# Hybrid block kernel: the second half of the modulation is summed on VectorE, and ScalarE evicts every projection result

## What is computed

```
m = silu(cond) @ w_ada + b_ada          # cond: two vectors, w_ada: 1024 x 6144
sh1, sc1, g1, sh2, sc2, g2 = split(m, 6)
h = rmsnorm(x, norm_mix) * (1 + sc1) + sh1
gq, gk, gv, gg, glr, sq, sk, sv = split(h @ w_in)      # 1024 x 2848
g_f, g_b = log_sigmoid(glr @ w_gk + b_gk) / 16         # gates, then running sums
sq, sk = rotary(rmsnorm(sq)), rotary(rmsnorm(sk))
x = x + g1 * merge(gla(gq, gk, gv, g_f, g_b), gg, attention(sq, sk, sv))
h = rmsnorm(x, norm_ff) * (1 + sc2) + sh2
x = x + g2 * (relu(h @ w_ff1) ** 2 @ w_ff2)
```

## Time and profile before

| | |
|---|---|
| runs of the kernel before, median of 3 | 1648.76 us (1645.47 to 1649.05) |
| the profiled execution, its own time | 1647.43 us |
| span of the profiled execution | 1645.7 us |
| projection stage, about | 40 to 388.4 us of the span |
| TensorE busy over the span | 1588.2 us (97%) |
| VectorE busy over the span | 973.5 us (59%) |

### The profile page before, as it was taken

The page is one execution under the profiler, slowest core; times in us unless marked ns, Lnnn a source line. Parts: engine busy times, 40 slices in busy tenths (PEclk is TensorE's granted clock), DMA queues, the critical chain, the costliest instruction groups (busy, mean ns, idle before and its releaser), DMA issues.

```text
span 1645.7 us, 31938 instructions
## 1 busy us (share of the span) xinstructions
PE 1588.2 (97%) x11618; PEld 1391.1 (85%) x11618; DVE 973.5 (59%) x1503; ACT 687.3 (42%) x1212; POOL 1019.1 (62%) x784
## 2 busy tenths in 40 slices
PE   4999999998999999999999999999999999999998
PEld 1999778897788877788889899998979899998987
DVE  2713564775665665457866656666694545545468
ACT  2513323324454566213444444444535444444441
POOL 1711455573485799103777777687898767676673
PEclk7999999999999999999999999999999999999999
DMA  8344555749655763334743132331344132231313
GB/s 323 109 131 165 187 181 191 264 143 257 195 162 171 230 179 114 147 130 155 215 167 103 51 102 63 90 95 58 103 132 150 52 102 73 80 102 51 102 52 115
DMA packets 211450, 225.93 MB, mean 137 GB/s; under 512 B 52752, under 2 KB 171664, under 8 KB 208144
## 3 DMA queue, kind: packets, MB, share of 16 engines
q1 hardware_dynamic: 209248, 224.46, 42.9%
q10 hardware_dynamic: 2096, 0.02, 0.1%
HBM read 177.22 MB, written 47.24 MB: 136 GB/s over the span
## 4 chain that ended last, share of the span: by engine, by line
PE 44%; POOL 4%; DVE 1%; issue 1%; ACT 0%; DMA 0%; SPq 0%; DVEq 0%; ACTq 0%; POOLq 0%
PE ff_banks L3189 8%; PE ff_banks L3190 8%; PE ff_banks L3191 8%; PE ff_banks L3162 7%; PE ff_banks L3164 7%; PE ff_banks L3163 7%; POOL h_whi L2835 1%; POOL h_xop L2432 1%; POOL h_wlo L2847 1%; POOL h_whi L2842 1%; DVE ff_tmp L3036 0%; DMA ff_hb<-in_w_ff 0%; DVE ff_acc L3026 0%; DVE ff_acc L2993 0%; POOL h_wlo L2882 0%
## 5 line engine op out<-in xcount | busy, mean ns | idle before, releaser
L3162 PE MATMUL ff_banks<-h_xop,h_whi 128*128 128x320 f32 x888 | 275.2, 310 | 4.6 <-POOL h_whi L2835 2.0
L3164 PE MATMUL ff_banks<-h_xop,h_whi 128*128 128x320 f32 x888 | 274.4, 309 | 0.0
L3163 PE MATMUL ff_banks<-h_xop,h_whi 128*128 128x320 f32 x888 | 274.3, 309 | 0.0
L2993 DVE TENSOR_TENSOR ff_acc<-ff_acc,ff_banks 128x512 f32<-128x512 f32 x296 | 200.6, 681 | 100.5 <-PE ff_banks L3191 98.9
L3189 PE MATMUL ff_banks<-h_wlo 128*128 128x512 f32 x580 | 226.5, 390 | 1.6 <-POOL h_whi L2842 0.8
L3191 PE MATMUL ff_banks<-h_wlo 128*128 128x512 f32 x580 | 225.6, 389 | 0.0
L2835 POOL TENSOR_TENSOR h_whi<-mid_raw,h_whi 128x512 fp32r<-128x512 f32 x149 | 208.4, 1415 | 1.4 <-ACT h_whi L2687 1.4
L2847 POOL TENSOR_TENSOR h_wlo<-mid_raw,h_wlo 128x320 fp32r<-128x320 f32 x128 | 116.7, 913 | 127.4 <-ACT mid_raw L2724 127.4
L3162 PEld LDWEIGHTS ff_banks<-h_xop,h_whi 128*128 128x128 f32 x888 | 166.7, 188 | 8.3 <-issue 3.6
L3163 PEld LDWEIGHTS ff_banks<-h_xop,h_whi 128*128 128x128 f32 x888 | 166.7, 188 | 1.1
L3164 PEld LDWEIGHTS ff_banks<-h_xop,h_whi 128*128 128x128 f32 x888 | 166.7, 188 | 0.0
(11 more groups left out here) (323 smaller groups left out, 3771.6 us busy)
## 6 DMA issues: line engine op xcount, KB each, us to landing
mid_raw<-in_w_ff SPq DMA_DIRECT2D x124, 512.0 KB, 4.4
mid_raw<-in_w_ada SPq DMA_DIRECT2D x18, 1024.0 KB, 7.2
early_room<-qk_by_channel SPq DMA_DIRECT2D x20, 512.0 KB, 4.2
proj<-prj_stage SPq DMA_DIRECT2D x60, 152.0 KB, 1.9
mid_raw<-in_w_in SPq DMA_DIRECT2D x6, 1216.0 KB, 7.3
early_room<-in_w_ada SPq DMA_DIRECT2D x6, 1024.0 KB, 11.1
decays<-early_room SPq DMA_DIRECT2D x8, 640.0 KB, 4.6
early_room<-decays SPq DMA_DIRECT2D x20, 256.0 KB, 2.9
```

The lines of the kernel that those rows point to most:

```text
L2993: dve.tensor_tensor(acc[:, p, at], acc[:, p, at], down[n % RING], ALU.add).then_inc(added, 1)
L3162: pe.matmul(out, w_hi[:, k], x_hi[:, k], start=(k == 0), stop=False)
L3163: pe.matmul(out, w_hi[:, k], x_lo[:, k], start=False, stop=False)
L3164: mm = pe.matmul(out, w_lo[:, k], x_hi[:, k], start=False, stop=(k == KH - 1))
```

## The change

The modulation's sixteen later slices are no longer multiplied on TensorE. Their 4096 columns are taken as four quarters of 1024 columns (u = 0 to 3: g1, sh2, sc2, g2). A quarter is loaded in four pieces of two slices (256 rows by 1024 columns, as many bytes as one slice before), two pieces in each of groups 2 to 9. For each slice and each of the two conditioning vectors VectorE multiplies 128 x 1024 weights with the vector's 128 values, one for each partition, and adds the product to a running sum (`dve_later`: 64 instructions, of which the 8 that begin a sum only multiply). When a quarter is complete, TensorE adds up the 128 partitions with a matrix that has one column of ones (`pe_sum`: four matmuls, after items 37, 49, 65 and 80). Rows, transposes and picks follow once for each quarter. All items from 10 on are evicted by ScalarE; `evacuate` is gone from VectorE.

```diff
+    def dve_later(self, dve, i, k, j, count):
+        u, q = i // 4, i % 4
+        dve.wait_ge(self.later_in[j], 16 * count)
+        for c in range(2):
+            t = 4 * i + 2 * k + c
+            by = self.silu[:, 2 * q + k, c:c + 1]
+            in_ = self.raw_slice(j)[:, 2 * k * HALF:(2 * k + 2) * HALF]
+            if t % 16 < 2:
+                if u:
+                    dve.wait_ge(self.sum_ready, u)
+                op = dve.tensor_scalar(self.sums[:, c], in_, by, None, ALU.mult)
+            else:
+                dve.wait_ge(self.product_ready, t - 1)
+                op = dve.scalar_tensor_tensor(self.sums[:, c], in_, by, self.sums[:, c], ALU.mult, ALU.add)
+            op.then_inc(self.product_ready, 1)
+
+    def pe_sum(self, pe, bank, u):
+        pe.wait_ge(self.picked, 3)
+        pe.wait_ge(self.product_ready, 16 * (u + 1))
+        if u:
+            pe.wait_ge(self.rows_ready, u + 1)
...
+        for c, j, row, at in self.places(u):
+            mm = pe.matmul(bank[row - c:row - c + 32, :], self.pick[:, c], self.sums[:, c, j * HALF:(j + 1) * HALF], start=True, stop=True)
+        mm.then_inc(self.sum_ready, 1)
...
-        slices = [(g, at) for g, places in ((2, (3, 7)), (3, (2, 5)), (4, (2, 5)), (5, (2, 5)), (6, (5,)), (7, (2, 5, 9)), (8, (1, 5, 9)), (9, (4,))) for at in places]
...
+        for g in range(2, NG):
+            for m, (load, first) in enumerate(((0, 1), (3, 4)) if by_channel(g) else ((-3, -1), (1, 3)) if g == NG - 1 else ((0, 2), (5, 7))):
+                i = 2 * (g - 2) + m
+                slice_load_at[FIRST_ITEM[g] + load] = i
+                for k in range(2):
+                    slice_at[FIRST_ITEM[g] + first + k] = (i, k)
...
+        sum_at = {FIRST_ITEM[4] + 1: 0, FIRST_ITEM[6] + 1: 1, FIRST_ITEM[8] + 1: 2, FIRST_ITEM[9] + 6: 3}
+        rows_at = {n + 1: u for n, u in sum_at.items()}
...
-        def on_act(n):
-
-            return n < NT or n % 2 == 1
...
                         if used_until[g - 1]:
-                            sp.wait_ge(ada.slice_used, KD + used_until[g - 1])
+                            sp.wait_ge(ada.product_ready, 4 * used_until[g - 1])
...
                     if n == max(heads_at) + 6:
-                        sp.wait_ge(ada.slice_used, 3 * KD)
+                        sp.wait_ge(ada.product_ready, 8 * KD)
...
-                        if on_act(n):
-                            evacuate(n)
+                        evacuate(n)
...
-                    elif not on_act(n):
-                        evacuate(n)
...
+                    if n in slice_at:
+                        i, k = slice_at[n]
+                        ada.dve_later(dve, i, k, slices[i] % 2, slice_count[i])
```

More of the change, by code:

```diff
@@ new lines, in dve_later_rows, with dve_later_pick @@
+    def dve_later_rows(self, dve, bank, u):
+        dve.wait_ge(self.sum_ready, u + 1)
+        dve.wait_ge(self.bias_in, 16 * 4 * (u + 2))
+        dve.tensor_tensor(self.rows[:, :], bank, self.rows[:, :], ALU.add).then_inc(self.rows_ready, 1)
+    def dve_later_pick(self, dve, bank, u):
+        cols = bank.rearrange("p (b j r) -> p j b r", j=4, r=32)
+        dve.wait_ge(self.cols_ready, u + 1)
+        for c in range(2):
+            src = cols[:, 2 * c:2 * c + 2, :, c]
+            if u == 1:
+                dve.tensor_copy(self.keep["shift"][:, 1].rearrange("p (j b) c -> p j b c", j=2)[:, :, :, c], src).then_inc(self.shift_ready, 1)
+            else:
+                gain = self.gain[:, 1].rearrange("p (j b) -> p j b", j=2)
+                dve.scalar_tensor_tensor(self.keep["scale"][:, 1].rearrange("p (j b) c -> p j b c", j=2)[:, :, :, c], src, 1.0, gain,
+                                         ALU.add, ALU.mult).then_inc(self.scale_ready, 1)
@@ L229, in dve_pick, with sp_store @@
                     dve.scalar_tensor_tensor(out[:, jj], src[:, jj], 1.0, gain, ALU.add, ALU.mult).then_inc(self.scale_ready, 1)
[L231 to L236, removed]
+    def sp_store(self, sp, u):
+        sp.wait_ge(self.rows_ready, u + 2)
+        for c, j, row, at in self.places(u):
+            sp.dma_start(self.scratch["mod"][c:c + 1, at:at + HALF], self.rows[row:row + 1, :]).then_inc(self.mod_out, 16)
 class HeadNorm:
@@ L763, in _ @@
                         i = slice_load_at[n]
-                        room = slices[i][0]
+                        room = slices[i]
                         sp.wait_ge(wlo_ready, room)
-                        sp.wait_ge(ada.slice_used, KD + (i if room == g else used_until[room - 2]))
-                        ada.sp_later(sp, 1 + i // KD, i % KD, room % 2)
+                        before = i if i % 2 else used_until[room - 2]
+                        if before:
+                            sp.wait_ge(ada.product_ready, 4 * before)
+                        ada.sp_later(sp, i, room % 2)
                     store(n)
```

102 lines of the change are left out of this document (51 added, 51 removed).

## The result

The changed kernel takes 1676.56 us in the median of five runs (1676.45 to 1678.31), against 1648.76 us before: ratio 1.0184, with a 95% interval of 1.0172 to 1.0197. It is 28 us slower; forecast were 13 us, and the range ended at 1674. One execution of the kernel before at 3292.3 us is left out of the comparison.

The account below looks back on a forecast made before the run. TensorE bounds the kernel overall, but VectorE is full in the projection's last groups. The stage would end at 401.5 us instead of 388.4, 13.1 us later: 1647.4 + 13.1 = 1660.5, against the median 1662; range 1647 to 1674.

Parts of the forecast that it names:

- The step that failed: Groups 2 to 6: VectorE's 40 products, some 45 us, roughly fit 56 us of waits; scan of item 53 at about 275.3.
- the way that the prediction had named itself: Around item 51: item 49's eviction 7.4 us earlier moves group 7's high and low parts; VectorE goes on at 268.1.
- the prediction's own signs of being wrong: Fourth sum finds products ready, products run at half of 1.2 us, or TensorE's idle ends on an eviction or weights' part.
- Late pieces: Group 9: pieces take 7.2 us to land, hidden behind some 12 us of VectorE work; if not, a few us at most.
- TensorE's part: Projection stage: sixteen slices, 17.05 us, go and four sums, 4.3 us, come; net 12.8 us less, the whole possible gain.
- shorter stops ... around items 51 and 65: TensorE at sums and transposes around items 51 and 65 to 67: stops of some us, taking only part of the same lag.
- VectorE full from item 53 to its last product: From the scan at 275.3 us VectorE works 113.6 us without a wait for data or TensorE; last product at 388.9.
- The last sum and behind: TensorE idles 10 to 20 us before the fourth sum, then 1.1 + 10.0 + 1.5 us to the stage's end at 401.5.
- Evictions at nothing: ScalarE's 37 more evictions, 5 us more in the last three groups, cost nothing, since TensorE has four banks.
- SyncE's loads for mixing at nothing: Loads for the mixing stage wait for the last product, then some 9 us of issuing fit under TensorE's last 11 us.
- The rule on ports: Two-input VectorE and GpSimd SBUF instructions exclude each other; at most 16 us more beside products, of which none was taken.
- the rule taken strictly: In the full stretch, five tiles' products meet GpSimd's short work, at most 16 us more: 1662 + 16 = 1678 us.

Follow-up runs that it names:

- e2: The changed kernel, but products read a resident tile and don't wait for the pieces, which are still loaded at their old places: 1662.54 us, ratio 1.0096.
- e6: The changed kernel, but the 32 products of groups 2 to 5 take only 128 of 1024 columns: 1659.29 us, ratio 1.0074.
- e12: The changed kernel with the low parts of groups 5 and 6 moved right behind prj_rstd of the second and third heads tile on GpSimd: 1678.24 us, ratio 1.0195.
- e11: The kernel before with only the low parts of groups 5 and 6 moved right behind prj_rstd on GpSimd: 1645.08 us, ratio 0.9994.
- e7: The changed kernel, but the 32 products of groups 6 to 9 take only 128 of 1024 columns: 1650.61 us, ratio 1.0021.
- e4: The kernel before with ScalarE evicting all items from 10 on and the slices left on TensorE: 1647.01 us, ratio 1.0001.
- e5: The changed kernel with the last quarter's sum on TensorE after item 83 instead of after item 80: 1676.08 us, ratio 1.0181.

## Why the prediction was wrong

**The step that failed** is the one that said: "From group 2 to 6 there are 40 products (some 45 us) against 56 us of waits and the evictions' time there ... so VectorE roughly keeps up", with the scan of item 53 at 275.3 us. It started at 288.1. I had set a sum of work against a sum of idle time. The products can't use that room at will: each stands at a place in the queue and waits for its piece, 31.5 us in all up to item 53 (21.2 of them ahead of the loop), and from 177 us on the pieces go out behind the next group's weights, which wait for the products. e2 takes the waits away and gives 275.6 us and 1662.5; e6 takes the length of the products away and gives 273.9 us. So neither cause does it alone. This is 12.8 us of the 14.3 us by which the stage's end (415.8 us) was missed.

The lag took the way that the prediction had named itself, from the eviction of item 49 by the high and low part of group 7 to `prj_ssq`, only in the other direction. Ahead of it TensorE had stopped 5.6 and 4.1 us for low parts, so the high part began at 271.14 us, where 259.1 were worked out (266.08 - 7.4 + 0.4); e2 has it at 259.57:

```profile
271.14 2.23 ACT L876 ACTIVATE prj_whi<-mid_raw 128x2432 fp32r<-128x2432 f32 x1
```

```profile
273.45 6.33 POOL L929 TENSOR_TENSOR prj_wlo<-mid_raw,prj_whi 128x2432 fp32r<-128x2432 f32 x1 [4.43 <-ACT prj_whi L876]
```

VectorE even waited 4.2 us for it, ahead of 281.03. But these stops aren't the root. In e12, where they are gone, the same step begins at 282.77 us without a wait: there VectorE's own queue is late, with two first products that take 6.53 us where 1.42 are usual, while the low part of group 7 runs (271.09 to 276.6 us):

```profile
270.62 6.53 DVE L228 TENSOR_SCALAR prj_ada_sums<-mid_raw,prj_ada_silu 128x1024 f32<-128x1024 f32 x2 [0.63 <-DMA mid_raw<-in_w_ada]
```

One of the prediction's own signs of being wrong thus came: idle time of TensorE that ends on a weights' part.

**Late pieces** I did cost, but only in group 9 ("hidden; if not, it is at most a few us"), and not in groups 3 to 5, where the trace of before showed nothing of VectorE waiting for a load. I had named the wait of the weights' load for the products and looked at one place of it alone, group 9's load at item 64.

**TensorE's part** was right in kind and too small: a slice frees 1.19 us and not 1.07, some 14 us in all. That the gain can be cashed ahead of item 54 was wrong. Low part 5 ended at 214.3 us before, and TensorE began group 5 here:

```profile
216.67 0.50 PE L982 MATMUL prj_banks<-h_hi,prj_whi 128*128 128x512 f32 x1
```

That is a slack of 2.4 us. (The 0.9 us in the expectation of e11 counts only to the end of the item before, ahead of a block of logits and a slice.) In the changed kernel TensorE is there at 210.6 us, 6.0 earlier, and the low part ends at 216.2, 1.9 later: 6.0 + 1.9 - 2.4 = 5.5, the stop of 5.6 us. More of it is time saved ahead of it that comes to nothing than lateness. The prediction spoke of "shorter stops ... around items 51 and 65" that only take part of the same lag; the two at groups 5 and 6 weren't among them.

**VectorE full from item 53 to its last product:** 113.6 us predicted, 114.1 measured, in part by luck. One product waited 1.1 us for its piece, and one pair of products, one row of four, one scan and one product for `keep_dec` took about 1 us longer each; against that `early_room`'s three operations of 1280 elements fell from 6.4 us to 4.4, the four copies to `keep_dec` from 2.3 to 0.7, and the wait of 1.1 us for `prj_rstd` went. A product takes 1277 ns in the median and 2.47 us in pairs, 1.22 us each in four (1.20 predicted); a first one 751 ns, 0.71 each in pairs (0.70). e7 shows the price from the other side: 26 us less with the late products narrow.

**The last sum and behind:** stop 14.1 us (10 to 20 predicted). From the last product to the end of item 83 it is 13.6 us against 12.6: the four matmuls take 1.93 us and not 1.1 because they run behind a stop, and matmuls of 304 columns start 0.25 us apart until about 407.4 us, at a granted clock of 0.50 (its lower level, 1.2 GHz), and 0.14 us from then on. That is 0.9 + 3.3 / 2 = 2.5 us for the restart, where 1.5 were predicted. Nothing behind the stage changed by more than executions differ.

**Evictions at nothing:** right (e4). **SyncE's loads for mixing at nothing:** right for the time, but close, as e5 shows.

**The rule on ports.** The Trainium skill, page "SBUF — State Buffer", section "Who interferes with whom", has a VectorE instruction with two SBUF inputs and a GpSimd instruction that reads SBUF exclude each other. The trace agrees that they meet. GpSimd's `prj_rstd`, to be held against the earlier trace rows, where the median is 1958 ns:

```profile
L513 POOL TENSOR_TENSOR prj_rstd<-prj_ms,keep_minus_half x10: 1952/2866/5558, 183.9 to 385.0; 128x10 f32<-128x10 f32 x10
```

and products, of which one ran into a low part from 168.83 us on:

```profile
L231 DVE SCALAR_TENSOR_TENSOR prj_ada_sums<-mid_raw,prj_ada_silu,prj_ada_sums x56: 1269/1277/5650, 129.9 to 400.9; 128x1024 f32<-128x1024 f32 x56
```

The time by the rule taken strictly was to be 1678 us, and 1676.6 came; but not by that route. In the full stretch 0.5 us were lost against the sum, not 16. Products do lengthen `prj_rstd` there, but VectorE never waits for it, and what products lost by meetings (about 2 us) other operations won. Ahead of item 53, where the lag arose, one meeting cost 5.4 us (169.43 us) and in e12 one of a product with a single input cost 5.1 us; the 16 us were worked out for the full stretch alone.

What stays open: how the lag of 12.8 us divides between the first late piece, the meeting with the low part and the turns of the loop; and whether some arrangement of pieces in groups 3 to 5, with another room than the weights', would let half of the change win its 6 us. That needs a buffer or an order that no run here had.

## What to carry to other kernels

Idle time of an engine isn't a sum to fill. Nor is busy time all that an instruction costs: a slice was busy for 1.07 us and held 1.19 us of TensorE's program. Ask for each added instruction when its data can be there at the earliest, what its completion releases, and whether that release feeds the next one's data; three places are enough to find a loop, and it has to be looked for in each group, not only in the last. And before a gain on the bound engine is counted, look at how much slack its inputs have: where a low part arrives 2.4 us before it is wanted, work taken off ahead of it is worth 2.4 us at most until that input comes earlier too. If taking one stop away brings another of the same length, the engine that feeds them is late, and moving waits won't help.

## What I had not expected of the hardware

Ten-element operations on GpSimd grow beside products of 1.3 us: `prj_rstd` went from 1.96 to 2.87 us in the median. Four matmuls of 512 columns on four separate column groups took 1.07 us at full clock but 1.93 us right after a stop of 14 us, and with the matmuls behind them the time to recover was 2.5 us and not 1.5.
